# Position bias folded into the selection mask, and two levels of a recurrence copied by ScalarE, in a one-core decoder trunk

## The chip, the cores and the metric

One core of one Trainium2 chip runs the whole program. The metric is the device time of one execution in microseconds (us), the median over three runs. About 0.2% of it, some 6 us, is what a measurement of this kernel can tell from no change. The engines are TensorE (PE, with its weight loads listed apart as PEld), VectorE (DVE), ScalarE (ACT), GpSimd (POOL) and SyncE (SP), which starts most of the DMAs.

## What is computed

The reference is a decoder trunk of two layers over 1040 tokens (16 meta tokens and 1024 of the input) of width 1024. The even layer mixes with two head groups side by side, and the change is in these. All the rest (output projection, layer norms, SwiGLU, pooling mixer) is untouched.

```python
# (A) sparse attention: an indexer picks 256 keys per query, 8 heads of 64
score = einsum(relu(q_idx . k_idx), w_idx); score = where(causal, score, -inf)
_, idx = top_k(score, 256)
logits = (q . k_sel) * 64 ** -0.5
logits = logits - slope[h] * (t - idx)        # slope[h] = 2 ** -(h + 1)
p = softmax(where(idx <= t, logits, -inf))
out_a = p . v_sel
# (B) gated linear recurrence, 8 heads of 64, chunkwise
S_t = exp(logf_t) * S_(t-1) + k_t (x) v_t;  out_b = q_t . S_t
```

A softmax over keys does not change when a constant is added to a whole row of logits. So the bias of a query at position t may be written as slope * (key - c) with any c for the row.

## The kernel before, in words

The work runs in three stages, each ended by a barrier of all engines: `projection`, `mixers` and `trunk`. Queries are cut into nine tiles: tile 0 has the 16 meta tokens, tiles 1 to 8 have 128 tokens each, and tile m sees `NKEYS[m]` keys (16, 144, 272, ..., 1040).

**projection.** PE computes the indexer scores, then column slabs of the input projection (L398 to L412). Meanwhile DVE takes the 256 best keys of tiles 2 to 7 out of the scores, eight at a time (L586 to L598), and turns what is left into a mask of 0 and -1e30 (L602). For each of these six tiles POOL then blanks the part above the diagonal (`causal`, called at L331). For tiles 0 and 1 it clears the scores near the start (L285). The stage ends when the last slab is stored (ACT, L492) and POOL is through.

**mixers.** The loop runs over 72 units, 8 for each tile m: the unit (m, h) is head h of the attention of tile m and level h of the recurrence of tile m. All engines walk the same list of steps, each in its own fixed order. In a unit:

- PE: `qk` gives the logits of the head in pieces of at most 512 keys. In each piece a product over two rows (`alibi` x `rel`, in type float32r, L1003) writes the bias, and the float32 product of queries and keys (L1005) is added to it. Each float32 product shows as two records in the trace. Then `gram` (L1048; level 0 is L1038) gives one level of the recurrence's scores, then come a job on the shared bank (output, state, turned outputs), the transposes of the probabilities of the unit before (`turn`, L1063), the product with the values of the one before that (`pv`, L1085), and at h = 1, 3, 5, 7 a quarter of the output projection (L996).
- DVE: `masked` (L1265) adds mask and logits in one pass and takes the row's maximum. `scores_of` copies the level's blocks from PSUM to `S` under a mask (`copy_predicated`, L1330 and L1336). Steps of the selection for tile 8 (L1364, L1375), of the normalisation (L1398, L1401) and of the layer norm fill the rest.
- ACT: the exponential of the logits (L1123), copies of the transposes (L1132, L1135), gates.
- POOL: `carry` (L892, L895) multiplies queries and keys by the decay of the level. `gram` of the next level waits for it.

PE's `qk(i)` waits for DVE's `masked(i-1)`; `gram` of level h waits for POOL's `carry` of level h-1 (L1044) and for the copy two levels back (L1031). PE's transposes of the normalised output (L975) wait for DVE's L1401.

Ahead of the loop POOL clears buffers (L842 to L857) and makes index rows, DVE builds the level masks (L1238 to L1244) and the two bias operands (L1234, L1235, L1246, L1248), and the gates of tile 0 run through ACT and DVE (L1151 to L1168, L1314). PE's first `qk` waits for `alibi_done` (L1013).

**trunk** is the rest of the network, on the same engines.

Of the kernel before, what the change touches and what calls it, by code (L numbers as in the profile page):

```python
# [6 lines left out]
F32R = mybir.dt.float32r  # L7
I32 = mybir.dt.int32
# [52 lines left out]
def scores_at(score, m, a, b):  # L61

    return score[1][:, a:b] if m == NT - 1 else score[0][:, SC_OFF[m] + a:SC_OFF[m] + b]

# [57 lines left out]
def projection(nc, c, sem, sb, banks, ident, x, meta, w_in_v, ins, score, cqT, kaT, va, y, qz_dram, vg_dram):  # L122
# [30 lines left out]

    cq_gain = sb(c, "cq_gain_sb", [P, QC])
# [33 lines left out]
    idx_hi, idx_lo = sem("w_idx_hi"), sem("w_idx_lo")  # L188
    stored = [sem(f"stored{i}") for i in range(NS)]
# [89 lines left out]
    def _(pool):  # L279
# [5 lines left out]
        nc.gpsimd.memset(score[0][:, 0:SC_OFF[FIRST_TOPK]], 0.0).then_inc(ident_zero, 1)  # L285
        pool.wait_ge(ident_zero, 2)
# [42 lines left out]
        for i, m in enumerate(EARLY):  # L329
            pool.wait_ge(mask_done, i + 1)  # L330
            causal(m, mask_all)  # L331
# [273 lines left out]
def mixers(nc, c, sem, sb, banks, ident, x, meta, ins, score, cqT, kaT, va, y, qz_dram, vg_dram):  # L605
# [25 lines left out]
    REL0 = TILES[-1][0]  # L631
    rel_f, rel_i = probs[0:2, 0, :], probs[0:2, 1, :].bitcast(I32)
    rel = sb(c, "rel", [2, L], F32R)
    qpos_i = sb(c, "qpos_i", [2, P], I32)
    qpos = sb(c, "qpos", [2, P])
    alibi = sb(c, "alibi", [2, A_HEADS, P], F32R)
# [31 lines left out]
    w_loaded, iotas, rel_done, alibi_done = sem("wqa_loaded"), sem("iotas"), sem("rel_done"), sem("alibi_done")  # L668
# [73 lines left out]
    def tails(i):  # L742

        return sum(m == NT - 1 for m, _ in units[:i + 1])

# [95 lines left out]
    def _(pool):  # L841
# [4 lines left out]

        nc.gpsimd.iota(rel_i, pattern=[[1, L]], base=-REL0, channel_multiplier=0).then_inc(iotas, 1)
        nc.gpsimd.iota(qpos_i[:, :], pattern=[[-1, P]], base=0, channel_multiplier=0).then_inc(iotas, 1)
        nc.gpsimd.memset(vt[:, 0, :], 0.0).then_inc(pads, 1)
        nc.gpsimd.memset(gt[:, :], 0.0).then_inc(pads, 1)  # L850
        pool.wait_ge(iotas, 4)
        nc.gpsimd.affine_select(out=rel_f, in_=rel_f, compare_op=ALU.is_ge, fill=1.0, base=0,
                                pattern=[[0, L]], channel_multiplier=-1).then_inc(rel_done, 1)
        nc.gpsimd.affine_select(out=qpos[:, :], in_=qpos[:, :], compare_op=ALU.is_gt, fill=1.0, base=0,
                                pattern=[[0, P]], channel_multiplier=1).then_inc(rel_done, 1)
# [55 lines left out]
        for i, (m, h) in enumerate(steps):  # L911
# [9 lines left out]
            if norm_tile(m, h, 5) is not None:  # L921
                n0.bias(pool, norm_tile(m, h, 5))
            if i == LATE1 + 1:
                pool.wait_ge(late_mask, 1)
# [1157 lines left out]
```

## Time and profile before

| | us |
|---|---|
| median of three runs (2826.09 to 2831.94) | 2829.19 |
| the profiled execution's own time | 2828.17 |
| its span in the trace | 2826.5 |
| PE busy / VectorE busy | 2670.7 / 1298.3 |
| ScalarE busy / GpSimd busy | 843.9 / 1055.6 |
| mean granted clock of TensorE, of full speed | 0.956 |

The profiled execution is 1.0 us under the median, and 1.7 us of it lie outside the span. Engines are busy side by side, so these numbers don't add up. The trace counts time in us from the start of the span. Projection runs to about 535, mixers to about 1138, trunk to the end. "Released by" in a row (the arrow) names the instruction that ended a wait.

### The profile page before, as it was taken

The numbers are of one execution on the slowest core, as the hardware profiler recorded it, in microseconds if no ns is written. First come the engines' busy times: TensorE is split into PE (matmuls) and PEld (weight loads), VectorE is DVE, ScalarE is ACT, GpSimd is POOL, SyncE is SP. The second block draws the span as 40 slices with busy tenths as digits, with TensorE's granted clock in tenths as the row PEclk, the third lists the DMA queues.
The fourth block names the chain that finished last, engine by engine and source line by source line (L and its number), as shares of the span: only waits on it lengthen the run. The fifth ranks groups of instructions, "written<-read, shape, count | busy, mean of one in ns | idle before, by whom it ended". The sixth has DMA issues, their size and how long they took to land.

```text
span 2826.5 us, 36645 instructions
## 1 busy us (share of the span) xinstructions
PE 2670.7 (94%) x14423; PEld 2237.4 (79%) x14423; DVE 1298.3 (46%) x2480; ACT 843.9 (30%) x1377; POOL 1055.6 (37%) x628
## 2 busy tenths in 40 slices
PE   6779999689999998799999999999999999999996
PEld 5758999677777776688889877788877788888885
DVE  4889999756656542233333332232322232233224
ACT  2573222123332321332222232332332232233222
POOL 1221111354543331434333352444343344345433
PEclk8898999769999999899999998999999999999998
DMA  2001121213323213332233321333322333333331
GB/s 95 30 1 45 53 91 59 80 50 109 101 83 94 72 63 123 120 90 73 78 105 90 90 79 56 90 89 112 97 75 60 92 89 114 94 90 97 104 112 52
DMA packets 276469, 232.95 MB, mean 82 GB/s; under 512 B 10448, under 2 KB 257296, under 8 KB 276304
## 3 DMA queue, kind: packets, MB, share of 16 engines
q1 hardware_dynamic: 268112, 222.13, 26.3%
q10 hardware_dynamic: 8192, 8.52, 0.9%
q8 instruction: 115, 1.88, 0.3%
q14 instruction: 50, 0.41, 0.0%
HBM read 217.91 MB, written 12.71 MB: 82 GB/s over the span
## 4 chain that ended last, share of the span: by engine, by line
PE 56%; DMA 1%; POOL 1%; ACT 1%; DVE 1%; issue 0%; POOLq 0%; SPq 0%; ACTq 0%; DVEq 0%
PE banks L1783 33%; PE banks L1799 19%; PE banks L1816 1%; PE banks L1821 1%; PE banks L1833 1%; DMA draw<-in_w_down 1%; DMA raw<-in_w_up 1%; POOL wL L1702 0%; POOL dL L1709 0%; PE banks L1507 0%; ACT wH L1877 0%; ACT dH L1883 0%; DVE y L1485 0%; PE banks L1818 0%; DVE y L1983 0%
## 5 line engine op out<-in xcount | busy, mean ns | idle before, releaser
L1783 PE MATMUL banks<-hL,wH 128*128 128x512 f32 (+1 forms) x1760 | 620.0, 352 | 16.3 <-ACT hid L1892 14.5
L1702 POOL TENSOR_TENSOR wL<-raw,wH 128x2048 fp32r<-128x2048 f32 x88 | 406.5, 4619 | 593.8 <-ACT wH L1877 593.8
L1783 PE MATMUL banks<-hH,wL 128*128 128x512 f32 (+1 forms) x1760 | 619.0, 352 | 0.0
L1783 PE MATMUL banks<-hH,wH 128*128 128x512 f32 (+1 forms) x1760 | 616.8, 350 | 0.0
L1963 DVE TENSOR_TENSOR hid<-hid,banks 128x512 f32<-128x512 f32 (+1 forms) x110 | 64.4, 585 | 759.4 <-PE banks L1783 648.0
L1783 PEld LDWEIGHTS banks<-hL,wH 128*128 128x128 f32 x1760 | 332.3, 189 | 65.9 <-ACT hid L1892 16.0
L1783 PEld LDWEIGHTS banks<-hH,wL 128*128 128x128 f32 x1760 | 332.2, 189 | 46.3
L1783 PEld LDWEIGHTS banks<-hH,wH 128*128 128x128 f32 x1760 | 332.7, 189 | 45.0
L1709 POOL TENSOR_TENSOR dL<-draw,dH 128x1024 fp32r<-128x1024 f32 x88 | 220.8, 2509 | 373.1 <-ACT dH L1883 373.0
L1983 DVE TENSOR_TENSOR y<-y,banks 128x512 f32<-128x512 f32 (+1 forms) x340 | 233.2, 687 | 220.9 <-PE banks L1799 219.9
L1799 PE MATMUL banks<-dH,hidL 128*128 128x512 f32 (+1 forms) x748 | 304.6, 407 | 2.3 <-issue 2.3
L1799 PE MATMUL banks<-dL,hidH 128*128 128x512 f32 (+1 forms) x748 | 302.3, 404 | 0.0
L1799 PE MATMUL banks<-dH,hidH 128*128 128x512 f32 (+1 forms) x748 | 301.2, 403 | 0.0
L1883 ACT ACTIVATE dH<-draw 128x1024 fp32r<-128x1024 f32 x88 | 93.4, 1061 | 565.4 <-PE banks L1799 372.2
L892 POOL TENSOR_TENSOR qp<-qp,tot 64x256 f32<-64x256 f32 x126 | 88.7, 704 | 290.0 <-PE banks L1048 284.9
L1877 ACT ACTIVATE wH<-raw 128x2048 fp32r<-128x2048 f32 x88 | 167.9, 1908 | 41.9 <-DMA raw<-in_w_up 41.7
L1894 ACT ACTIVATE hidH<-hid 128x512 fp32r<-128x512 f32 (+1 forms) x110 | 60.5, 550 | 384.8 <-DVE hid L1963 384.8
L1799 PEld LDWEIGHTS banks<-dH,hidL 128*128 128x128 f32 (+1 forms) x748 | 141.3, 189 | 42.7 <-issue 4.3
L1799 PEld LDWEIGHTS banks<-dH,hidH 128*128 128x128 f32 (+1 forms) x748 | 141.2, 189 | 39.1
L1799 PEld LDWEIGHTS banks<-dL,hidH 128*128 128x128 f32 (+1 forms) x748 | 141.5, 189 | 36.8
L598 DVE MATCH_REPLACE8 y<-top,y 128x272 f32<-128x272 f32 (+2 forms) x192 | 143.4, 760 | 0.0
L410 PE MATMUL banks<-shared,hH 128*128 128x256 f32 (+1 forms) x648 | 137.1, 280 | 0.0
(231 smaller groups left out, 4373.0 us busy)
## 6 DMA issues: line engine op xcount, KB each, us to landing
raw<-in_w_gate SPq DMA_DIRECT2D x88, 512.0 KB, 4.8
raw<-in_w_up SPq DMA_DIRECT2D x88, 512.0 KB, 6.1
draw<-in_w_down SPq DMA_DIRECT2D x88, 512.0 KB, 3.5
w_out_part<-in_w_out SPq DMA_DIRECT2D x64, 512.0 KB, 3.9
slab<-in_w_in SPq DMA_DIRECT2D x10, 1024.0 KB, 5.8
va<-in_x SPq DMA_DIRECT2D x8, 512.0 KB, 5.1
vg_scratch<-y ACTq DMA_DIRECT2D x32, 128.0 KB, 1.7
y<-in_x SPq DMA_DIRECT2D x8, 512.0 KB, 7.2
```

The source lines that it names most:

```text
L410: last = nc.tensor.matmul(banks[0:n, i % 8, 0:SW], h[:, k, a:a + n], w[:, k, :], start=first, stop=stop)
L598: nc.vector.match_replace(at, top8[:, m, :], at, TAKEN).then_inc(topk_step, 1)
L892: nc.gpsimd.tensor_tensor(late, late, blocks[r, :, 0, :].to_broadcast([HD, n, 2 ** l]), ALU.mult) .then_inc(carried, 1)
L1702: nc.gpsimd.tensor_tensor(wL[:, ff % 2, :, :, :].rearrange("p g k f -> p (g k f)"), raw[:, :, :, :].rearrange("p g k f -> p (g k f)"), wH[ ...
L1709: nc.gpsimd.tensor_tensor(dL[:, ff % 2, :], draw[:, :], dH[:, ff % 2, :].bitcast(F32), ALU.subtract)\
L1783: last = nc.tensor.matmul(banks[:, GU + (2 * q + g) % 3, 0:n], wt[:, ff % 2, g, k, :], h[:, k, a:a + n], start=(k == 0 and part == 0), sto ...
L1799: last = nc.tensor.matmul(banks[0:n, DN + num % 3, :], h[:, (2 * g + u) % 3, t0 - ph.t0:t0 - ph.t0 + n], wt[:, u, (j % 2) * 512:(j % 2 + 1 ...
L1877: nc.scalar.activation(wH[:, ff % 2, :, :, :], raw[:, :, :, :], ACT.Copy).then_inc(w_hi, 1)
L1883: nc.scalar.activation(dH[:, ff % 2, :], draw[:, :], ACT.Copy).then_inc(d_hi, 1)
L1894: nc.scalar.activation(hidH[:, ff % 3, a - ph.t0:a - ph.t0 + n], hid[:, q % 2, 0:n], ACT.Copy)\
L1963: nc.vector.tensor_tensor(hid[:, q % 2, 0:n], hid[:, q % 2, 0:n], banks[:, GU + (2 * q + 1) % 3, 0:n], ALU.mult)\
L1983: nc.vector.tensor_tensor(at, at, banks[0:n, DN + num % 3, :], ALU.add).then_inc(y_added, 1)
```

## The change

The bias moves out of the product and into the mask. `dist` is a row 1-L, ..., -1, 0 on all partitions, and its last `NKEYS[m]` entries (`dist_of`) are key minus last query of the tile. It is added once per tile to the selection mask instead of once per head to the logits. The slope is taken out of the logits: the query weights are divided by it ahead of time, and the exponential multiplies by it (`scale`), as does the negated maximum. In tiles 0 and 1 the mask is `dist` itself.

- PE: L1003 is gone from every piece of every unit.
- projection: POOL makes `dist` (one iota, one cast of 128x1040), copies it for tiles 0 and 1, and adds it to the masks of tiles 2 to 7 at the stage's end (L344 of the new file).
- mixers, start: POOL and DVE no longer make the bias operands. ACT scales the query weights in eight instructions, and PE's first product waits for these.
- mixers, loop: POOL makes `dist` again after unit 8 and adds it to the mask of tile 8 at unit 62.
- Levels 6 and 7 of `scores_of` go from DVE to ACT (`blocks_of`): the blocks are whole squares there, so plain copies do (two of 32 partitions, then one of 64).

```diff
@@ projection, POOL
-        nc.gpsimd.memset(score[0][:, 0:SC_OFF[FIRST_TOPK]], 0.0).then_inc(ident_zero, 1)
-        pool.wait_ge(ident_zero, 2)
+        nc.gpsimd.iota(dist[:, :].bitcast(I32), pattern=[[1, L]], base=1 - L, channel_multiplier=0).then_inc(dist_done, 1)
+        pool.wait_ge(dist_done, 1)
+        nc.gpsimd.tensor_copy(dist[:, :], dist[:, :].bitcast(I32)).then_inc(dist_done, 1)
+        pool.wait_ge(dist_done, 2)
+        for m in range(FIRST_TOPK):
+            nc.gpsimd.tensor_copy(scores_at(score, m, 0, NKEYS[m]), dist_of(dist, m)).then_inc(dist_done, 1)
+        pool.wait_ge(dist_done, 2 + FIRST_TOPK)
...
         for i, m in enumerate(EARLY):
             pool.wait_ge(mask_done, i + 1)
+            at = scores_at(score, m, 0, NKEYS[m])
+            nc.gpsimd.tensor_tensor(at, at, dist_of(dist, m), ALU.add).then_inc(placed, 1)
+            pool.wait_ge(placed, i + 1)
             causal(m, mask_all)
@@ mixers, POOL
-        pool.wait_ge(iotas, 4)
...
+            if i == A_HEADS:
+                nc.gpsimd.iota(dist[:, :].bitcast(I32), pattern=[[1, L]], base=1 - L, channel_multiplier=0).then_inc(dist_done, 1)
+                pool.wait_ge(dist_done, 1)
+                nc.gpsimd.tensor_copy(dist[:, :], dist[:, :].bitcast(I32)).then_inc(dist_done, 1)
             if i == LATE1 + 1:
+                pool.wait_ge(dist_done, 2)
                 pool.wait_ge(late_mask, 1)
+                nc.gpsimd.tensor_tensor(late, late, dist_of(dist, NT - 1), ALU.add).then_inc(late_placed, 1)
+                pool.wait_ge(late_placed, 1)
@@ mixers, PE
-        pe.wait_ge(w_loaded, 16)
+        pe.wait_ge(w_scaled, A_HEADS)
...
         def scores_of(m, h, a, kn, at):
             t0, n = TILES[m]
-            nc.tensor.matmul(logits[0:n, at:at + kn], alibi[:, h, 0:n], rel[:, REL0 - t0 + a:REL0 - t0 + a + kn],
-                             start=True, stop=False)
             return nc.tensor.matmul(logits[0:n, at:at + kn], qaT[:, m % 2, h, 0:n], kaT[:, h // 2, a:a + kn],
-                                    start=False, stop=True)
+                                    start=True, stop=True)
@@ mixers, ACT
+        act.wait_ge(w_loaded, 16)
+        for h in range(A_HEADS):
+            at = w_qa[:, :, h * HD:(h + 1) * HD]
+            nc.scalar.activation(at, at, ACT.Copy, scale=HD ** -0.5 / SLOPES[h]).then_inc(w_scaled, 1)
...
-            nc.scalar.activation(at, at, ACT.Exp, bias=nmax[0:n, i % 2, 2:3], accum_out=sums[0:n, m % 2, h:h + 1])\
+            nc.scalar.activation(at, at, ACT.Exp, bias=nmax[0:n, i % 2, 2:3], scale=SLOPES[h], accum_out=sums[0:n, m % 2, h:h + 1])\
...
+        def blocks_of(i):
+
+            m, h = units[i]
+            l = h - 1
+            act.wait_ge(gram_psum, i + 1)
+            act.wait_ge(gram_read, i)
+            for b in range(P // 2 ** h):
+                r = slice(b * 2 ** h, b * 2 ** h + 2 ** l)
+                src = banks[r, GRAM + h % 2, :].rearrange("p (h n t) -> p h n t", h=8, t=2 ** l)[:, :, b, :]
+                last = nc.scalar.activation(S[r, m % 2, :, b * 2 ** h + 2 ** l:(b + 1) * 2 ** h], src, ACT.Copy)
+            last.then_inc(gram_read, 1)
...
+            if i < NU and h in PLAIN:
+                blocks_of(i)
@@ mixers, DVE
-        dve.wait_ge(iotas, 2)
-        nc.vector.tensor_copy(rel_f, rel_i).then_inc(iotas, 1)
-        nc.vector.tensor_copy(qpos[:, :], qpos_i[:, :]).then_inc(iotas, 1)
...
-        dve.wait_ge(rel_done, 2)
-        linked(nc.vector.tensor_copy(rel[:, :], rel_f))
-        for h in range(A_HEADS):
-            last = nc.vector.tensor_scalar(alibi[:, h, :], qpos[:, :], 2.0 ** (-8.0 * (h + 1) / A_HEADS), None, ALU.mult)
-        last.then_inc(alibi_done, 1)
...
-            if i < NU:
+            if i < NU and h not in PLAIN:
```

How the order of the instructions changes is shown at three places. In the rows the name of a line is that of its own file.

On PE, a unit of tile 7 in the mixers loop (`w_out_part` is the output projection's quarter, `kaT` and `qaT` are keys and queries, `qp` and `key` the recurrence's operands, `ident` marks transposes), before:

```order
L996 MATMUL banks<-w_out_part,oT 128x256 x8
L1003 MATMUL banks<-rel,alibi 128x512
L1005 MATMUL banks<-kaT,qaT 128x512
L1003 MATMUL banks<-rel,alibi 128x400
L1005 MATMUL banks<-kaT,qaT 128x400
L1048 MATMUL banks<-qp,key 128x128 x4
L979 MATMUL banks<-ident,o_tok 128x128 x4
```

and with the change:

```order
L1010 MATMUL banks<-w_out_part,oT 128x256 x8
L1017 MATMUL banks<-kaT,qaT 128x512
L1017 MATMUL banks<-kaT,qaT 128x400
L1058 MATMUL banks<-qp,key 128x128 x4
L993 MATMUL banks<-ident,o_tok 128x128 x4
```

The two bias products are gone, and float32 products follow one another from the quarter of the output projection to the recurrence's.

On DVE, the start of the mixers stage, from the last level mask to the first gate (`pT` holds index tables there), before:

```order
L1241 TENSOR_SCALAR pT<-pT 128x128
L1242 SCALAR_TENSOR_TENSOR masks<-pT 128x128
L1244 TENSOR_SCALAR masks<-pT 128x128
L1246 CAST rel<-probs 2x1040
L1248 TENSOR_SCALAR alibi<-qpos 2x128 x8
L1314 SCALAR_TENSOR_TENSOR key_arg<-zt,lnw 128x512
L1317 SCALAR_TENSOR_TENSOR lnw<-zt,lnw 128x512
```

and with the change:

```order
L1265 TENSOR_SCALAR pT<-pT 128x128
L1266 SCALAR_TENSOR_TENSOR masks<-pT 128x128
L1268 TENSOR_SCALAR masks<-pT 128x128
L1332 SCALAR_TENSOR_TENSOR key_arg<-zt,lnw 128x512
L1335 SCALAR_TENSOR_TENSOR lnw<-zt,lnw 128x512
```

Nine instructions ahead of the first gate are gone, and two casts (L1234, L1235) at the head of this queue.

On POOL, the end of the projection stage (`y` holds the scores there), before:

```order
L308 TENSOR_TENSOR slab1L<-slab,shared 128x2048
L291 AFFINE_SELECT y<-y 128x128 x6
L86 UNCONDITIONAL_BRANCH
L88 ISA
L840 UNCONDITIONAL_BRANCH
L842 MEMSET zt 128x512
```

and with the change:

```order
L320 TENSOR_TENSOR slab1L<-slab,shared 128x2048
L344 TENSOR_TENSOR y<-y 128x272
L303 AFFINE_SELECT y<-y 128x128
L344 TENSOR_TENSOR y<-y 128x400
L303 AFFINE_SELECT y<-y 128x128
L344 TENSOR_TENSOR y<-y 128x528
L303 AFFINE_SELECT y<-y 128x128
```

Six adds, of 272 to 912 elements a partition (3552 together), now stand between the masks and the stage's end.

## Rows read from the trace of the kernel before

**Rows 1.** busy time by stage: stretch, PE PEld DVE ACT POOL busy, PEclk, DMA, GB/s

```profile
586.90:648.40 61.50, 58.79 (x300) 47.28 (x300) 34.84 (x70) 16.12 (x55) 32.58 (x49) 0.67 0.13 39
648.40:1087.40 439.00, 434.13 (x2606) 334.13 (x2607) 237.76 (x465) 136.19 (x339) 177.55 (x233) 1.00 0.27 84
```

**Rows 2.** waits on PE, 550:1090; columns: who for whom, total, times, longest

```profile
PE banks L1003 <- DVE alibi L1248: 11.2, 1, 11.2
PE banks L1048 <- POOL key L895: 9.9, 5, 3.0
```

**Rows 3.** line L1003 on PE: its forms, and its busy time in the stage

```profile
L1003 PE MATMUL banks<-rel,alibi x120: 168/445/501, 553.5 to 1083.7; 2*128 2x512 f32 x48, 2*128 2x144 f32 x16, 2*128 2x272 f32 x16, 2*128 2x400 f32 x16
...
550.00:1150.00 600.00, 48.96 (x120) 21.66 (x120) 0.93 0.28 88
```

**Rows 4.** timeline of PE, one unit of tile 7 (start, us, what)

```profile
951.71 0.49 PE L1003 MATMUL banks<-rel,alibi 2*128 2x512 f32 x1
952.13 1.13 PE L1005 MATMUL banks<-kaT,qaT 128*128 128x512 f32 x2
953.19 0.44 PE L1003 MATMUL banks<-rel,alibi 2*128 2x400 f32 x1
953.56 0.94 PE L1005 MATMUL banks<-kaT,qaT 128*128 128x400 f32 x2
954.34 1.07 PE L1048 MATMUL banks<-qp,key 128*128 128x128 f32 x8
```

**Rows 5.** timeline of PE, 1087:1091

```profile
1087.40 3.62 PE L996 MATMUL banks<-w_out_part,oT 128*128 128x256 f32 x16
1090.86 1.04 PE L1063 MATMUL banks<-ident,probs 128*16 128x128 f32 x8
```

**Rows 6.** timelines of DVE, POOL and ACT, start of the mixers stage

```profile
539.99 7.38 DVE L1241 TENSOR_SCALAR pT<-pT 128x128 int32<-128x128 int32 x1
...
551.51 0.69 DVE L1246 CAST rel<-probs 2x1040 fp32r<-2x1040 f32 x1
...
553.32 0.67 DVE L1314 SCALAR_TENSOR_TENSOR key_arg<-zt,lnw 128x512 f32<-128x512 f32 x1
...
536.87 0.98 POOL L847 IOTA probs<- 2x1040 int32 x1
...
539.75 1.11 POOL L852 TENSOR_SCALAR_AFFINE_SELECT probs<-probs 2x1040 f32<-2x1040 f32 x1 [0.23 <-DVE qpos L1235]
...
545.49 1.79 POOL L857 MEMSET qp<- 128x2048 f32 x1
...
544.75 0.63 ACT L1158 ACTIVATE lnw<-u 128x512 f32<-128x512 f32 x1
```

**Rows 7.** timelines of ACT and POOL around the stage's end, then a POOL group

```profile
532.65 0.33 ACTq L492 DMA_DIRECT2D vg_scratch<-y  x1
...
523.91 2.74 POOL L291 TENSOR_SCALAR_AFFINE_SELECT y<-y 128x128 f32<-128x128 f32 x6 [35.03 <-DVE y L602]
535.55 0.53 POOL L842 MEMSET zt<- 128x512 f32 x1 [8.91 <-POOLq L89]
...
L1491 POOL TENSOR_TENSOR y<-y,n_b 128x1024 f32<-128x1024 f32 x6 | 14.1, 2354 | 18.9 <-DVE y L1485 18.9
```

**Rows 8.** masked copies of L1336 on DVE (ns min/median/max)

```profile
L1336 DVE COPY_PREDICATED S<-masks,banks x63: 675/726/1327, 560.5 to 1084.8; 128x512 f32<-128x512 uint8 x63
```

**Rows 9.** timelines of POOL and PE, tile 2

```profile
655.56 0.74 POOL L895 TENSOR_TENSOR key<-key,tot 128x256 f32<-128x256 f32 x1
...
656.45 1.13 PE L1048 MATMUL banks<-qp,key 128*128 128x128 f32 x8
```

**Rows 10.** timelines of DVE and PE, tile 4

```profile
777.95 0.69 DVE L1401 TENSOR_TENSOR on<-on,gt 128x512 f32<-128x512 f32 x1
...
778.79 0.63 PE L975 MATMUL banks<-ident,on 128*128 128x128 f32 x4
```

**Rows 11.** timeline of PE, tile 1

```profile
591.61 2.08 PE L1048 MATMUL banks<-qp,key 128*128 128x128 f32 x8
```

More of the change, by code:

```diff
@@ L63, in scores_at, with dist_of @@
     return score[1][:, a:b] if m == NT - 1 else score[0][:, SC_OFF[m] + a:SC_OFF[m] + b]
+def dist_of(dist, m):
+    return dist[:, L - NKEYS[m]:L]
 def key_chunks(n):
@@ L152, in slab_raw @@
         return slab_first[:, j, :, :] if j < 2 else slab[:, j % 2, :, :]
+    dist = y[:, 3:5, :].rearrange("p m f -> p (m f)")[:, 0:L]
     cq_gain = sb(c, "cq_gain_sb", [P, QC])
@@ L188, in projection @@
     idx_hi, idx_lo = sem("w_idx_hi"), sem("w_idx_lo")
+    dist_done, placed = sem("dist_done"), sem("placed")
     stored = [sem(f"stored{i}") for i in range(NS)]
@@ L630, in mixers @@
     o_tok = sb(c, "o_tok", [P, 2, A_WIDTH])
[L631 to L636, printed above, removed]
+    dist = sb(c, "dist", [P, L])
+    SLOPES = [2.0 ** (-8.0 * (h + 1) / A_HEADS) for h in range(A_HEADS)]
     zt = sb(c, "zt", [P, W])
@@ L666, in mixers @@
     rsh = sb(c, "rsh", [P, 8])
-    w_loaded, iotas, rel_done, alibi_done = sem("wqa_loaded"), sem("iotas"), sem("rel_done"), sem("alibi_done")
+    w_loaded, w_scaled, late_placed = sem("wqa_loaded"), sem("wqa_scaled"), sem("late_placed")
+    dist_done = sem("late_dist_done")
     qk_done, qk_tail, nmax_raw, nmax_tail, nmax_done = (sem("qk_done"), sem("qk_tail"), sem("nmax_raw"),
@@ L744, in tails @@
         return sum(m == NT - 1 for m, _ in units[:i + 1])
+    PLAIN = (LEVELS - 1, LEVELS)
     def halves(ap, l):
@@ L845, in _ @@
         nc.gpsimd.iota(it_t, pattern=[[1, P]], base=0, channel_multiplier=0).then_inc(iota_done, 1)
-        nc.gpsimd.iota(rel_i, pattern=[[1, L]], base=-REL0, channel_multiplier=0).then_inc(iotas, 1)
-        nc.gpsimd.iota(qpos_i[:, :], pattern=[[-1, P]], base=0, channel_multiplier=0).then_inc(iotas, 1)
         nc.gpsimd.memset(vt[:, 0, :], 0.0).then_inc(pads, 1)
         nc.gpsimd.memset(gt[:, :], 0.0).then_inc(pads, 1)
-        pool.wait_ge(iotas, 4)
[L852 to L855, printed above, removed]
         for dst in (qaT, S, state, added, qp):
@@ L1011, in qk @@
                 pe.wait_ge(shared_done, nth["qa", m])
-            if i == 0:
-                pe.wait_ge(alibi_done, 1)
             if i:
@@ L1179, in off_shared @@
                     to = qaT[r, m % 2, :, 0:n].rearrange("p (f two) t -> p two f t", two=2)[:, par]
-                    ins_ = nc.scalar.activation(to, four(src)[r, :, 0:n], ACT.Copy, scale=HD ** -0.5)
+                    ins_ = nc.scalar.activation(to, four(src)[r, :, 0:n], ACT.Copy)
             if what == "kT":
@@ L1277, in masked @@
                 peak = 1
-            nc.vector.tensor_scalar(nmax[0:n, i % 2, 2:3], nmax[0:n, i % 2, peak:peak + 1], -1.0, None, ALU.mult)\
+            nc.vector.tensor_scalar(nmax[0:n, i % 2, 2:3], nmax[0:n, i % 2, peak:peak + 1], -SLOPES[h], None, ALU.mult)\
               .then_inc(nmax_done, 1)
```

## The prediction

> **What bounds the kernel now.** I first cut the trace by stage. The change touches only what lies before 1138 us, so the trunk, 1688 us of the span, is taken as it is. Within the mixers the table of busy time [rows 1] shows PE busy 58.8 of 61.5 us in tile 1 and 434.1 of 439.0 us in tiles 2 to 8, while DVE has work for 54% and POOL for 40% of the latter. Busy PE proves little, since records overlap. So I looked at the waits: from 550 to 1090 us PE waited 11.2 us for the bias operands, once, ahead of the first unit, and 9.9 us for POOL's decays, five times [rows 2], all in tile 0. The timeline of a unit says the same: each PE instruction starts where the one before lets it, with no gap but those that the weight loads make [rows 4]. So from tile 1 on the order on PE is the clock of the stage, and an instruction taken off PE is worth its whole distance to the next one. In tile 0 the loop runs PE, POOL, PE, and PE has time to spare.
>
> **The bias products.** There are 120 of them, 48.96 us busy [rows 3]. A record overlaps the next one: the piece of 512 is recorded with 0.49 us, but the next instruction starts 0.42 us after it [rows 4], 0.07 less. 48.96 - 120 x 0.07 = 40.6 us, less the eight of tile 0 that PE's waits hide (about 1 us): **40 us** if nothing but these distances goes. That is the lower bound.
>
> More may go. The 512 keys of L1005 take 952.13 to 953.19, 1.06 us, and the whole unit's logits 951.71 to 954.34, 2.63 us for 912 keys [rows 4]. Where float32 products follow each other without a float32r one in between, eight of 256 columns (16 records) take 1087.40 to 1090.86, 3.46 us, or 0.43 us for 256 columns [rows 5]; by that rate 912 columns take 1.54 us. The unit then saves 1.09 us, where the two distances of L1003 give 0.42 + 0.37 = 0.79. The rest is weight loads which the change of type seems to leave in the open, before and after each bias product. Scaled by 1.09/0.79 the 40 us become **55 us**. The entry into the first bias product of a unit may hide another 0.1 us in each of 64 units: 61 us, the upper bound. I take 55, since the rate of rows 5 is one of the same type on the same engine at the same clock.
>
> The Trainium skill, "TensorE: Matmul & The Clock Gate", table at the head: the queue of TensorE can pull a weight load ahead of matmuls in flight. Rows 5 agree with that, rows 4 don't at the two changes of type; if the rule held there too, the gain would be nearer 40 than 55.
>
> **What comes late next.** Two other engines get close to PE. POOL's decays: in tile 2 L895 ends at 656.30 and PE's product on it starts at 656.45 [rows 9], so in such units (some seven in tiles 1 to 3, those without a long job on PE) the saving of about 0.5 us is lost in part: -2 us. DVE's normalisation: in tile 4 L1401 ends at 778.64 and PE's transposes start at 778.79 [rows 10], the same 0.15 us that stands for a release. There the saving of the two units before is lost in part: 1 to 1.5 us in each of tiles 1, 4 and 5, -3.5 us. In tile 8 PE waits for DVE's maximum in each unit, and DVE will be late in a few: -1.5 us. Together 7 us given back, so 48 of the 55 arrive.
>
> **The start of the mixers.** DVE's first shift (L1241) lasted 539.99 to 547.37, where the fourteen instructions behind it take 4.1 us together, and it ended with POOL's run of memsets, at 547.28 [rows 6]: it got through only when POOL paused. POOL now does without an iota of 0.98 us and a select of 1.11 us [rows 6], two short ones of the same kinds and the wait for DVE between them, about 1 us more. Its memsets end at about 544.2. From the end of the first shift to L1246 DVE takes 551.51 - 547.37 = 4.1 us, which stays; from L1246 to L1314 it takes 1.8 us, which goes [rows 6]. So the first gate starts at 548.4 in place of 553.32: **-4.9 us**. All the chain of tile 0 hangs on this gate. What could fill the place: ACT's eight scalings of the query weights. They are 128 elements each in a row of 512-element instructions at 0.63 us [rows 6], so between 2 us (a third of that each, near what 128 elements should need) and 5 us for all. ACT's last gate ended at 545.38 and now ends up to 2 to 4 us later, since PE's product for the first queries comes behind the scalings; at 2 it is hidden, at 4 it costs 1 us. I take it as hidden.
>
> The Trainium skill, "SBUF — State Buffer", section "Who interferes with whom": GpSimd and a two-port DVE instruction lock each other out for one whole instruction. The trace shows more: the 7.38 us outlast four of five memsets. By the rule the shift would wait for one memset, 1.8 us, the masks would be through before ACT's gates, and the gain here would be about 6 us, not 4.9.
>
> **The end of the projection.** POOL's adds cost 2354 ns per 1024 elements [rows 7], so 3552 elements take 8.2 us, the six selects 2.7 as before [rows 7], and six hand-overs about 0.15 each. From 523.9 that ends at 535.7. Before, the last store was issued at 532.65 and POOL's first instruction of the next stage came at 535.55 [rows 7]; with some 2 us for the store to land, the barrier takes about 0.9. POOL is now last by about 1 us: **+1.2 us** (0 to +3). If the slabs did not cover it the price would be all 9 us.
>
> **Priced at nothing.** POOL's `dist` at the program's start lies ahead of its first long instruction, which waits for the indexer's weights; in the loop it lies behind unit 8 and at unit 62, where POOL is idle half the time; if that cover went, each would delay one decay by 2 to 3 us. The copies of levels 6 and 7: DVE loses 18 of about 0.73 us [rows 8], 13 us, but PE doesn't wait for them. ACT gets about 1.3 us in two units of each tile and is 31% busy [rows 1]. Behind its copies wait the transposed probabilities, which PE reads a whole unit later (3.5 us or more). If that cover went, it would be at most 9 x 1.3 = 12 us, and as a gain I see none: 0.
>
> **Sum.** 55 - 7 + 4.9 - 1.2 = 51.7. 2828.17 - 51.7 = 2776.5; the median stood 1.0 higher than this execution, so I forecast **2777 us** for the median.
>
> **Rivals.**
>
> - *Only the distances go, and the neighbours hold the rest.* The weight loads stay in the open and DVE and POOL take back 10 us: 40 - 10 + 4 - 2 = 32, so 2797. For it: two engines with 40 to 54% of work in fixed orders, and releases of 0.15 us already seen in two places. Against it: rows 5. Chance 0.22.
> - *The low clock holds on: slower.* The granted clock is 0.67 from 586.9 to 648.4, although PE is busy nearly throughout, and 1.00 after [rows 1]; at the low level (1.2 GHz) eight records of L1048 take 2.08 us, at the high one (2.4 GHz) 1.07 [rows 11, 4]. The bias products are work for PE; without them tiles 1 to 3 have less in the same order, and the rise at 648 could come later. Each us of PE's work done at the low level costs up to one more. The point from which it decides: some 52 us of work, that is the low level held through tile 2. Held through tile 3 (100 us of work) it gives 2777 + 80, about 2850. Against it: the shorter units pack the remaining products denser. The Trainium skill, "TensorE: Matmul & The Clock Gate", "What's actually happening", has the clock follow how busy PE has been; by that alone PE should have been at the high level in tile 1, and it wasn't. Chance 0.03.
> - *The clock rises earlier.* 0.67 over 61.5 us leaves about 20 us to be won in tile 1; half of it gives 2767. Chance 0.07.
> - *The parts cancel, or the bias products cost nothing*: in the trace nothing hides them from tile 1 on. Chance 0.01.
>
> **How the numbers follow.** Forecast 0.67, the rivals as above. The forecast's own range is 61 - 5 + 6 = 62 to 40 - 7 + 2 = 35, so 2766 to 2793; with most of the first rival and half of the clock's gain it becomes 2760 to 2800. Faster by over 0.2% (about 6 us, what a measurement can tell) 0.96, within 0.01, slower 0.03.
>
> **What would show it.** L1003 absent; a unit of tile 7 with its 912 keys in 1.5 to 1.6 us; L1048 and L975 with more waits, a few us in all; the first gate on DVE at about 549.5; the stage's first POOL instruction at about 536.7; the high clock from about 640. It is wrong if the logits' distance per unit shrinks by 0.8 us or less, if PE's waits in tiles 1 to 8 grow by over 12 us, if the low level outlasts tile 1, or if the trunk's length changes.

## The result, and the profile after

The changed kernel takes 2786.1 us (median of four runs, 2781.0 to 2788.7) beside 2827.6 us for the kernel before: ratio 0.9849, 95% interval 0.9829 to 0.9869. It is 41.5 us faster, where 52 were forecast: the forecast was 2777, 9 us under the result, and the kernel before came out 1.6 us lower with its fourth run. The range of 2760 to 2800 holds the result. The profiled execution took 2784.3 us.

The page of the changed kernel, its busy time (PE had 2670.7 before):

```profile
span 2782.6 us, 36417 instructions
...
PE 2620.8 (94%) x14303; PEld 2224.0 (80%) x14303; DVE 1284.3 (46%) x2451; ACT 854.9 (31%) x1412; POOL 1067.2 (38%) x636
```

PE lost 49.9 us of busy time and the span only 43.9. To see where, I cut both traces at the same events: the first gate (L1314 before, L1332 now), the first product of the logits of each tile, and the first PE instruction of the trunk. Tile 8 is taken up to the first product of its last unit, so seven of its eight units. The table is worked out from the start times of those rows.

| us | before | after |
|---|---|---|
| first gate starts at | 553.3 | 548.1 |
| gate to trunk | 585.2 | 546.0 |
| trunk | 1688.0 | 1688.5 |
| tile 1 | 51.6 | 44.7 |
| tile 2 | 48.0 | 49.1 |
| tile 3 | 51.3 | 51.5 |
| tiles 4 to 7 | 267.8 | 237.3 |
| tile 8, seven units | 73.7 | 69.8 |

The loop gave 39.1 us and what lies ahead of it 5.3. Tiles 4 to 7 gave 30.5 of the loop's, tiles 2 and 3 nothing, and seven units of tile 8, which has the most keys, 3.9, less than half of the 9.3 of tile 7.

Busy time by stretch, tile 1 and then tiles 2 to 8 of the changed kernel (columns as in [rows 1], whose first stretch runs on into tile 2):

```profile
583.20:627.90 44.70, 40.63 (x217) 33.76 (x216) 24.78 (x51) 14.89 (x51) 30.49 (x47) 0.70 0.10 28
627.90:1035.70 407.80, 394.72 (x2537) 328.30 (x2537) 237.58 (x461) 143.56 (x361) 180.74 (x235) 0.98 0.30 93
```

PE's granted clock was 1.00 in [rows 1] from 648.4 on. Now it is 0.98 over tiles 2 to 8: some of the time is at the low level (1.2 GHz). PE is also idle more. Its waits from 550 to 1090 us, changed kernel, answering [rows 2]:

```profile
PE banks L1058 <- POOL key L902: 11.5, 8, 3.0
PE banks L989 <- DVE on L1419: 11.2, 6, 3.4
PE banks L1017 <- DVE nmax L1283: 5.1, 8, 1.1
PE banks L1010 <- DMA w_out_part<-in_w_out: 4.4, 3, 2.0
...
PE banks L1073 <- ACT pT L1149: 1.0, 2, 0.5
```

The alibi wait is gone, POOL's decays stand at 11.5 us for 9.9, and the normalised output at 7.8 us in place of 2.7: the other 3.4 of the 11.2 stand behind the loop, and the kernel before has the same 3.4 there, outside the window of [rows 2]. The last line is new, and small. ScalarE's new order, from which it comes, will turn out to go with the largest loss.

A unit of tile 7 on PE, the counterpart of [rows 4]:

```profile
919.05 1.69 PE L1017 MATMUL banks<-kaT,qaT 128*128 128x512 f32 x4
920.58 1.07 PE L1058 MATMUL banks<-qp,key 128*128 128x128 f32 x8
```

One row holds both pieces: 919.05 to 920.58, 1.53 us for 912 keys. It was 2.63.

The start of the mixers, changed kernel: DVE, POOL and ACT, the counterpart of [rows 6] and of the POOL rows of [rows 7]:

```profile
538.90 0.32 DVE L1265 TENSOR_SCALAR pT<-pT 128x128 int32<-128x128 int32 x1
...
539.58 1.46 DVE L1265 TENSOR_SCALAR pT<-pT 128x128 int32<-128x128 int32 x1
...
541.40 1.46 DVE L1265 TENSOR_SCALAR pT<-pT 128x128 int32<-128x128 int32 x1
...
548.06 0.69 DVE L1332 SCALAR_TENSOR_TENSOR key_arg<-zt,lnw 128x512 f32<-128x512 f32 x1 [0.61 <-ACT lnw L1172]
...
533.11 2.10 POOL L344 TENSOR_TENSOR y<-y 128x912 f32<-128x912 f32 x1
535.36 0.29 POOL L303 TENSOR_SCALAR_AFFINE_SELECT y<-y 128x128 f32<-128x128 f32 x1
536.84 0.52 POOL L856 MEMSET zt<- 128x512 f32 x1 [1.19 <-POOLq L94]
...
539.08 1.88 POOL L864 MEMSET qaT<- 128x2048 f32 x1
540.90 1.87 POOL L864 MEMSET S<- 128x2048 f32 x1
...
540.14 1.70 ACT L1128 ACTIVATE w_qa<-w_qa 128x128 f32<-128x128 f32 x8 [2.01 <-DMA w_qa<-in_w_uq]
```

POOL ends the projection stage now and its first memset comes at 536.84 (535.55 in [rows 7]). DVE's shifts are no longer shut out for 7.38 us: each takes 1.46 us at most beside a memset of 1.88, and then gets through. The gate now waits 0.61 us for ACT, so ACT is what sets it.

The masked copies that stay on DVE, and the block copies on ACT, against [rows 8]:

```profile
L1354 DVE COPY_PREDICATED S<-masks,banks x45: 681/722/1336, 555.2 to 1021.1; 128x512 f32<-128x512 uint8 x45
```

```profile
L1223 ACT ACTIVATE S<-banks x27: 356/374/590, 578.6 to 1041.2; 32x256 f32<-32x256 f32 x18, 64x512 f32<-64x512 f32 x9
```

In tile 2 PE, DVE and POOL of the changed kernel stand like this, where [rows 9, 10] had shown releases of 0.15 us:

```profile
657.00 1.05 PE L1058 MATMUL banks<-qp,key 128*128 128x128 f32 x8
659.77 0.63 PE L989 MATMUL banks<-ident,on 128*128 128x128 f32 x4 [1.71 <-DVE on L1419]
...
660.66 1.47 PE L1095 MATMUL banks<-va,pT 16*128 16x64 f32 x6
662.06 4.79 PE L1010 MATMUL banks<-w_out_part,oT 128*16 128x256 f32 x16
...
656.43 1.52 DVE L1416 TENSOR_TENSOR on<-on,rsh 128x512 f32<-128x512 f32 x1
657.99 1.63 DVE L1419 TENSOR_TENSOR on<-on,gt 128x512 f32<-128x512 f32 x1
...
656.37 1.04 POOL L913 TENSOR_TENSOR state<-state,tot 128x512 f32<-128x512 f32 x1
657.49 1.59 POOL L915 TENSOR_TENSOR state<-state,state_added 128x512 f32<-128x512 f32 x1
```

DVE's two products took 1.5 and 1.6 us beside POOL's (0.69 in [rows 10], without them), PE waited 1.71 us, and right behind that wait its products ran slow: the quarter of the output projection took 4.79 us, where [rows 5] have 3.62. So this wait cost more than its length. Not every such wait does: in e6 below the same wait of 1.71 us stands in tile 2, and the tile ran at a granted clock of 1.00. The Trainium skill, "SBUF — State Buffer", section "Who interferes with whom", says that a DVE instruction with two inputs in SBUF contends with a GpSimd instruction that reads SBUF; these rows agree.

### The profile page after: what moved, and what is told of

It is laid out like the page before. It is cut to its first block, busy times and chain, and to the rows that moved or that the text cites. A ratio compares the mean times of both kernels' runs of the same rounds, so it can differ in the third digit from the quotient of the medians.

```text
span 2782.6 us, 36417 instructions
## 1 busy us (share of the span) xinstructions
PE 2620.8 (94%) x14303; PEld 2224.0 (80%) x14303; DVE 1284.3 (46%) x2451; ACT 854.9 (31%) x1412; POOL 1067.2 (38%) x636
## 4 chain that ended last, share of the span: by engine, by line
PE 56%; DMA 1%; POOL 1%; ACT 1%; DVE 1%; issue 0%; POOLq 0%; SPq 0%; ACTq 0%; DVEq 0%
PE banks L1801 34%; PE banks L1817 19%; PE banks L1834 1%; PE banks L1839 1%; PE banks L1851 1%; DMA draw<-in_w_down 1%; DMA raw<-in_w_up 1%; POOL dL L1727 1%; POOL wL L1720 0%; PE banks L1525 0%; ACT wH L1895 0%; ACT dH L1901 0%; DVE y L1503 0%; PE banks L1836 0%; DVE y L2001 0%
```

## The experiments

Twelve kernels ran, in three groups, each group on a chip of its own. All ratios are to the kernel before, timed on the same chip at the same time; its median was 2830.4 us for e0, e1, e5 and e6, 2827.2 for e2, e3, e8 and e9, and 2829.7 for e4, e10, e11 and e12. So medians of different groups can't be set against each other to within 3 us. Gate and loop (gate to trunk) are from each profile.

| run | median us | ratio, 95% interval | gate | loop | tiles 2, 3, 8 |
|---|---|---|---|---|---|
| e0_after_again | 2782.9 | 0.9832 [0.9814, 0.9850] | 549.0 | 545.9 | 49.1, 51.6, 69.8 |
| e1_bias_only | 2777.7 | 0.9808 [0.9790, 0.9826] | 549.0 | 538.6 | 48.5, 49.3, 64.7 |
| e5_on_first | 2776.1 | 0.9814 [0.9793, 0.9836] | 548.7 | 535.6 | 47.2, 49.3, 65.0 |
| e6_adds_dve | 2778.0 | 0.9811 [0.9791, 0.9831] | 545.4 | 545.3 | 48.1, 51.5, 69.8 |
| e2_blocks_only | 2828.7 | 1.0003 [0.9994, 1.0012] | 552.8 | 589.2 | 48.0, 51.3, 78.8 |
| e3_bias_f32 | 2925.9 | 1.0343 [1.0325, 1.0361] | 552.7 | 684.6 | 49.6, 55.2, 95.0 |
| e4_bias_twice | 2849.0 | 1.0068 [1.0053, 1.0084] | 552.0 | 610.3 | 48.4, 52.7, 81.9 |
| e10_rows128 | 2800.5 | 0.9897 [0.9882, 0.9913] | 553.1 | 556.6 | 47.5, 50.2, 67.9 |
| e9_turned_first | 2776.9 | 0.9818 [0.9804, 0.9831] | 547.7 | 538.2 | 48.5, 49.3, 64.7 |
| e8_all_three | 2774.6 | 0.9814 [0.9801, 0.9828] | 546.2 | 544.0 | 46.5, 48.6, 64.7 |
| e11_turned_adds | 2770.0 | 0.9798 [0.9783, 0.9813] | 544.5 | 537.9 | 47.3, 49.3, 64.7 |
| e12_turned_adds_on | 2775.3 | 0.9818 [0.9803, 0.9833] | 545.2 | 537.9 | 46.7, 48.6, 64.7 |

**e0_after_again** is the changed kernel itself.

> The changed kernel once more, as the mark for the others on the same chip. Expected 2781 to 2789 us. If the low clock in tiles 2, 3 and 8 belongs to the program, the 64-column products of tile 8 take the double time again; if it is chance, they don't, and the time is up to 5 us lower.

2782.9 us, and the tiles agree with the first profile to 0.1 us. The slow stretches in tiles 2, 3 and 8 belong to the program.

**e1_bias_only**: the changed kernel with levels 6 and 7 back on DVE.

```diff
-            if i < NU and h in PLAIN:
-                blocks_of(i)
...
-            if i < NU and h not in PLAIN:
+            if i < NU:
```

> The bias part alone: levels 6 and 7 stay masked copies on VectorE. Theory (the gain is the bias products alone, VectorE has room there): within 3 us of the changed kernel, and TensorE's waits for ScalarE's transposed probabilities (1.0 us) go. Rival 1 (ScalarE's copies hold up the transposed probabilities): faster by 4 us or more. Rival 2 (VectorE's relief pays): slower by 5 us or more, with more waits for VectorE in tiles 1 to 5.

5.2 us faster than the repeated change. The intervals of the two ratios overlap, but not the runs (2774.0 to 2779.1 and 2781.1 to 2785.3). In the profile the loop is 7.3 us shorter, in tiles 2, 3 and 8. The copies on ScalarE, which I had priced at nothing, cost in the place where they stand.

**e5_on_first**: the normalisation (L1416, L1419) right behind the maximum on DVE, the rest as changed.

> The changed kernel with VectorE's two normalisation steps of a tile right behind the maximum of the logits instead of at the unit's end. Theory (what was given back in tiles 1 to 5 is TensorE's wait for these steps, 7.8 us, and the low clock that follows the longest of them, 2 to 3 us): 7 to 10 us faster than the changed kernel, no wait for L1419 but the one after the loop, units 5 of tiles 2 and 3 in 8 us instead of 10.3. Rival (the next thing in the queue takes its place: gates, copies of blocks or of transposes late): 0 to 3 us, with new waits of the same sum.

6.8 us faster by the median, though its runs (2771.1 to 2785.2) spread over those of e0; the profile is of the fastest. PE's waits for the normalised output fell from 11.2 to 3.4 us (what is left stands behind the loop), tile 1 from 44.7 to 41.3, and the slow stretches of tiles 3 and 8 are gone too, with ScalarE's copies still in place. PE still waits twice for `pT` here:

```profile
PE banks L1073 <- ACT pT L1149: 1.0, 2, 0.5
```

A new wait of 3.9 us for ACT's `oT` and 2.5 us more in tiles 4 and 5 take a part back.

**e6_adds_dve**: the six adds of `dist` to the masks on DVE, behind its last mask.

> The changed kernel with the six adds of positions to the masks on VectorE behind the masks instead of on GpSimd. Theory (GpSimd was last at the stage's end by 1.3 us): the mixers stage starts at 535.5 as before the change instead of 536.8, the whole is 1 to 2 us faster, which only the trace can tell. Rival (something else ends that stage): it starts at 536.8 again.

4.9 us faster than the repeated change; the first gate comes 3.5 us earlier, the loop is the same. So POOL's adds at the stage's end cost some 3 us: 3.5 in this pair of profiles, 2.7 by the means given below.

**e2_blocks_only**: the kernel before with ScalarE's copies alone.

> The kernel before, with levels 6 and 7 of the recurrence's scores copied as whole blocks by ScalarE; the bias products stay. My theory, from the last runs: in the changed kernel these copies cost about 5 us, and chiefly because PE then slips to the low clock in tiles 3 and 8, which needs the lighter load that the missing bias products leave. Then here, where PE is loaded more, they cost little: between -2 and +3 us against the kernel before (2828 to 2833), tile 8 at 73 to 75 us. Rival 1: the copies cost by their place in ScalarE's order (the transposed probabilities come later in two units of each tile), whatever the clock does: +5 us or more here too, spread over the tiles. Rival 2: they gain here, since DVE's maximum ends earlier and PE waits for it in tile 8: -3 us or more.

2828.7 beside 2827.2: no difference. But my reason fell. In the profile, which is of the slowest of the eleven runs (2832.9), tile 8 did slip to the low clock (78.8 us for 73.7), without any lighter load on PE and without any wait of PE for `pT`. Tile 1 was shorter, 46.8 us for 51.6. That is no gain of the copies: tile 1 took 47.4 us in e4 and 51.2 in e3, where nothing was moved to ScalarE. Whether tile 8 slips in the other ten runs too is not shown.

**e9_turned_first**: the same work on ScalarE in another order.

```diff
-            if i < NU and h in PLAIN:
-                blocks_of(i)
             if 1 <= i <= NU:
                 turned(i - 1)
                 if units[i - 1][0] == NT - 1:
                     turned_rest(i - 1)
+            if i < NU and h in PLAIN:
+                blocks_of(i)
```

> The changed kernel with ScalarE's block copies moved behind the copies of the transposed probabilities, in the same two units of each tile. The work on ScalarE is the same, only its order differs. Theory 1: the copies cost what they cost because the transposed probabilities stand behind them and PE waits for them (0.5 us in a unit, and what the clock makes of it): then the waits for the transposed probabilities go, and the time falls by 3 to 5 us, to 2778 to 2780. Theory 2: it is the copies' contention or the earlier idle moments of PE that matter, not this order: 2782 to 2784, with tile 8 still at about 69.8 us. Theory 3: PE now waits for the copied blocks instead, in the product that reads level 6 or 7: 2785 or more.

2776.9 us. That is 6.0 less than the repeated change, but on another chip: by the two ratios it is 4 us, and their intervals overlap, so the times alone don't settle it. The profile does for the tiles: 2, 3 and 8 are those of e1 to the tenth. Theory 1 holds so far: not the copies cost, their place does. Nor does it gain anything that VectorE is rid of 18 copies: e9 and e1 take the same time. ACT and PE of the changed kernel, tile 2:

```profile
670.81 0.74 ACT L1223 ACTIVATE S<-banks 32x256 f32<-32x256 f32 x2
671.58 0.27 ACT L1146 ACTIVATE pT<-banks 16x128 f32<-16x128 f32 x1
671.75 0.36 ACT L1149 ACTIVATE pT<-banks 128x256 f32<-128x256 f32 x1
...
672.25 0.49 PE L1073 MATMUL banks<-ident,probs 128*16 128x128 f32 x3 [0.49 <-ACT pT L1149]
```

and of e9_turned_first at the same place:

```profile
670.41 0.25 ACT L1146 ACTIVATE pT<-banks 16x128 f32<-16x128 f32 x1
670.57 0.36 ACT L1149 ACTIVATE pT<-banks 128x256 f32<-128x256 f32 x1
670.84 0.74 ACT L1223 ACTIVATE S<-banks 32x256 f32<-32x256 f32 x2
...
671.21 0.49 PE L1073 MATMUL banks<-ident,probs 128*16 128x128 f32 x3
```

The next transposes write over the bank that `pT` is copied out of (`pe.wait_ge(t_act, i)` in `turn`), so a late copy holds PE. That happens twice, 0.49 and 0.51 us in tiles 2 and 3. Of the 8.0 us between the two kernels in these tiles (0.6 in tile 2, 2.3 in tile 3, 5.1 in tile 8) only 1.0 is this wait; nearly all the rest is PE at the low level. In tile 8, columns as before, the changed kernel:

```profile
972.00:988.00 16.00, 15.49 (x80) 13.54 (x80) 3.62 (x8) 3.89 (x7) 2.53 (x3) 0.70 0.00 1
...
977.80 0.39 PE L982 MATMUL banks<-state,qp 128*128 128x64 f32 x2
...
978.88 0.64 PE L982 MATMUL banks<-state,qp 128*128 128x64 f32 x2
```

and e9_turned_first over the same 16 us, in which it is 3.3 us further on in the program:

```profile
972.00:988.00 16.00, 14.48 (x99) 12.66 (x100) 7.01 (x17) 3.09 (x7) 4.70 (x6) 1.00 0.21 66
```

PE falls to the low level in the middle of a job of products of 64 columns, 0.39 us a pair and then 0.64. Up to there the two kernels' PE rows agree to 0.01 us in length for 25 us back, waits included. So putting the order right removed the low clock in tile 8, but no row near it shows what brings it on.

The short waits for `pT` are not enough to bring it. e5 has both of them (0.48 and 0.51 us) with the same order on ScalarE, and its tiles 3 and 8 ran at 1.00. e2 has the low clock in tile 8 and no such wait. The profiles of the change, e0, e6 and e2 have the low clock in tile 8; those of the kernel before, e1, e5 and e8 to e12 don't; e3 and e4, whose bias products are longer or doubled, have some of it with the old order (0.53 from 1074 to 1085 us in e4, in tile 8). In tile 3 the low stretch of the change lies ahead of that tile's wait for `pT`, behind one of 1.18 us for the normalised output at 710.05 (0.83 granted from 710 to 720); the same wait is in e9 (1.17 us, at 709.01), whose clock stayed at 1.00. What brings the low clock on stays open.

**e3_bias_f32, e4_bias_twice, e10_rows128** ask why a bias product cost more than its columns. All three are the kernel before with one edit:

```diff
@@ e3: float32 in place of float32r
-    rel = sb(c, "rel", [2, L], F32R)
-    alibi = sb(c, "alibi", [2, A_HEADS, P], F32R)
+    rel = sb(c, "rel", [2, L])
+    alibi = sb(c, "alibi", [2, A_HEADS, P])
@@ e4: each bias product twice
+            for again in range(2):
+                nc.tensor.matmul(logits[0:n, at:at + kn], alibi[:, h, 0:n], rel[:, REL0 - t0 + a:REL0 - t0 + a + kn],
+                                 start=True, stop=again == 0)
@@ e10: 128 rows in place of 2, the others zero
+    rel = sb(c, "rel", [P, L], F32R)
+    alibi = sb(c, "alibi", [P, A_HEADS, P], F32R)
...
+        linked(nc.vector.memset(rel[:, :].bitcast(mybir.dt.float32), 0.0))
+        linked(nc.vector.memset(alibi[:, :, :].bitcast(mybir.dt.float32), 0.0))
```

> The kernel before, with the two operands of the bias product in float32 in place of float32r: the same 120 products, but no change of type between them and the products of queries and keys. Theory: a float32r product between float32 ones lays weight loads open before and after it, about 0.2 us each; a float32 product of two rows costs twice the columns' time but no such load. Then in the unit of tile 7 the piece of 512 keys is 0.87 us long instead of 1.06, its bias product about 0.85 instead of 0.42, the unit's logits about 3.1 us instead of 2.63, and the whole about 20 to 30 us slower than before. Rival: the type has nothing to do with it, and any further product of other weights costs its load: then the 512 keys stay at 1.06 us, the unit's logits are about 3.4 us, and the whole is 40 us or more slower.

Part of a unit of tile 6 in e3_bias_f32:

```profile
952.50 1.12 PE L1003 MATMUL banks<-rel,alibi 2*128 2x512 f32 x2
953.55 1.13 PE L1005 MATMUL banks<-kaT,qaT 128*128 128x512 f32 x2
954.61 0.72 PE L1003 MATMUL banks<-rel,alibi 2*128 2x272 f32 x2
```

Without any change of type the 512 keys still take 1.06 us (953.55 to 954.61). My cause, the change of type, is refuted. The bias product in float32 takes 1.05 us (952.50 to 953.55) where 0.85 was expected, so it too costs 0.2 us beyond its columns. The whole is 98.7 us slower, in the open range of the rival (40 or more) and far above the theory's 20 to 30. A good part of it is this:

```profile
740.00:1085.00 345.00, 345.00 (x1707) 250.20 (x1707) 153.36 (x286) 83.82 (x201) 110.51 (x150) 0.88 0.22 70
```

PE is busy in all of these 345 us, waits for nobody, and is granted 0.88. In the kernel before the same tiles ran at 1.00. Twelve hundredths of 345 us are 41 us, my estimate of what the clock took; the rest is the longer products.

> The kernel before, with each bias product issued twice (the second starts the sum anew, so the values are the same): 120 more products over two rows, and none of them stands at a change between two rows and 128. What it tells apart is why a bias product cost more than its columns: 512 columns at four passes are 0.85 us, and the product of queries and keys took 1.06 although in the changed kernel it takes 0.85. Theory A (a product whose weights have another number of rows than those before it can't have its load pulled ahead; the float32 run has ruled out the type): two products over two rows follow each other at the columns' rate, so the second is 0.21 to 0.25 us for 512 columns, the first stays at 0.42, and the whole is 120 x 0.2 = 15 to 25 us slower than before. Theory B (every such product has its load in the open): the second takes 0.42 us as well, and the whole is 40 us or more slower.

The first piece of a unit of tile 6 in e4_bias_twice, two bias products (in one row) and the product of queries and keys:

```profile
929.85 0.73 PE L1004 MATMUL banks<-rel,alibi 2*128 2x512 f32 x2
930.50 1.13 PE L1006 MATMUL banks<-kaT,qaT 128*128 128x512 f32 x2
```

0.65 us for two where one took 0.42 [rows 4], so the second, which has the same two rows as the one ahead of it, adds 0.23; theory B wanted 0.84 for the two. The second has the same weights too, but it is not spared its load: the trace has 240 weight loads for the 240 products. The whole is 19.3 us slower, within the 15 to 25 of theory A.

> The kernel before, with the two operands of the bias product widened from 2 to 128 rows, the other 126 all zero: the same 120 products in float32r, with the same columns and the same sum, now over as many rows as the products of queries and keys. It adds two fills on DVE (about 2 us) at the start of the mixers, ahead of the first gate. Theory A (the change in the number of rows lays the loads open): in the unit of tile 7 the bias product of 512 keys takes 0.21 to 0.25 us in place of 0.42, the product of queries and keys 0.87 in place of 1.06, the unit's logits 1.9 to 2.0 us in place of 2.63, and the whole is 20 to 35 us faster than before, so half or more of what the change won in the loop comes without removing a single product. Theory B (the load of any further product is in the open): the unit's logits stay at 2.6 us or grow, and the whole is 0 to 5 us slower.

A unit of tile 7 in e10_rows128:

```profile
931.98 0.58 PE L1003 MATMUL banks<-rel,alibi 128*128 128x512 f32 x1
932.40 1.02 PE L1005 MATMUL banks<-kaT,qaT 128*128 128x512 f32 x2
...
934.10 1.08 PE L1048 MATMUL banks<-qp,key 128*128 128x128 f32 x8
```

2.12 us (931.98 to 934.10) in place of 2.63, a little more than the 1.9 to 2.0 expected, and the whole 29.2 us faster than before, with all 120 products still there. The single pieces don't start as expected (0.42 us from the bias product to the next, where 0.21 to 0.25 was expected); the unit and the whole do come out. The weight loads of the same rows show what changed. The kernel before [rows 4], then e10_rows128:

```profile
951.71 0.18 PEld L1003 LDWEIGHTS banks<-rel,alibi 2*128 2x128 f32 x1 [0.33 <-issue]
952.13 0.30 PEld L1005 LDWEIGHTS banks<-kaT,qaT 128*128 128x128 f32 x2 [0.24 <-issue]
```

```profile
931.95 0.19 PEld L1003 LDWEIGHTS banks<-rel,alibi 128*128 128x128 f32 x1
932.16 0.42 PEld L1005 LDWEIGHTS banks<-kaT,qaT 128*128 128x128 f32 x2
```

Before, each of these loads starts only when its product's own record starts (951.71 and 952.13, as in [rows 4]). With 128 rows the load for the keys starts at 932.16, 0.24 us ahead of its product at 932.40 and while the bias product runs. Theory A holds: a product over two rows among products over 128 has its weight load, and that of the next one, in the open. Only 2 and 128 rows were tried. The Trainium skill, "TensorE: Matmul & The Clock Gate", section "The mechanism", says in one place that a load overlaps a product in flight only when the two are in different groups of rows, and in another that the weight buffer in the background serves as well. The rows here are against the first: loads hide between products over the same 128 rows (the load at 932.16) and are laid open where the number of rows changes; the measurement decides.

**e8_all_three, e11_turned_adds, e12_turned_adds_on** put the single gains together: e8 is e1, e5 and e6 in one, e11 is e9 and e6, e12 is e11 and e5.

> The changed kernel with three edits that each gained alone: levels 6 and 7 back on DVE as masked copies, the normalisation on DVE right behind the maximum, the six adds of the distances on DVE. If the gains add up (5.1, 6.7 and 4.7 us over the repeated change): 2782.9 - 16.5 = 2766. Theory: the first two both work by keeping PE at the high clock in tile 8, so that gain counts once: 2782.9 - 5.1 - 6.7 - 4.7 + 5 = about 2771. Rival: with DVE's 18 masked copies back, the normalisation in front of them puts the copies late and PE waits for them: 2774 to 2778.

> The changed kernel with two edits: ScalarE's block copies behind the transposed probabilities (alone 2776.9) and the six adds of the distances on DVE (alone 4.7 us under the repeated change; the first gate 3.5 us earlier). They act in different places, the order in the loop and the stage's start, so they should add up: 2776.9 - 3.5 to 4.7 = 2772 to 2773.5, with tile 8 at 64.7 us and the first gate at about 545.5. Rival: the earlier start ends in tile 1 at the low clock, which then lasts longer: 2775 to 2777.

> The run before this one with the normalisation on DVE right behind the maximum too. That edit alone made tile 1 3.4 us and tile 2 2.0 us shorter and tiles 4 and 5 2.5 us longer in all; what it won in tiles 3 and 8 is already had. If this holds: 2772.5 - 2.9 = about 2769.5. Rival: DVE no longer copies levels 6 and 7 here, so the losses of tiles 4 and 5 go as well: 2767. Other rival: with the earlier start the gain in tile 1 is not repeated, as in the run with all three edits, where tiles 4 and 5 took 59.5 and 60.3 us: 2773 or more.

e8: 2774.6, within its rival's range, but hardly for its reason. Tiles 4 and 5 are 59.5 and 60.3 us long (55.5 and 57.4 in the change). 1.0 and 1.5 us of that stand in e5 and e12 as well (56.5 and 58.9), with the wait for `oT`; the rest goes with the low clock, 0.94 and 0.97 granted in e8 and 1.00 in e12. e11: 2770.0, a little better than expected, with the gate at 544.5. e12: 2775.3, not the 2769.5 expected. Its loop is as long as e11's (537.9): tiles 1 to 3 won 2.2 us and tiles 4 and 5 lost 2.5. The 5 us between the medians are thus not in the loop. The trunks of the two profiles differ by 4 us, and I have no reason for that; the same trunk took 1684.8 to 1691.9 us in the fourteen profiles, and 1684.8 and 1688.5 in the two of the changed kernel itself. **e11_turned_adds** is the fastest version that ran: 57 us under the kernel before by its ratio, and 10 to 14 under the change, by the ratio of e0 or of the first result.

## Why the prediction was right in kind and 9 us short

- **What bounds the kernel.** Right. The order on PE is the clock of the loop, and L1003 gave its distance and more.
- **The bias products, 55 us.** The size was right, the cause wrong. The unit of tile 7 takes 1.53 us, forecast 1.54 by the rate of [rows 5]. With ScalarE's order put right (e9) the loop is 47.0 us shorter than before, against 55 - 7 = 48. So close an agreement is part luck: tile 1 alone took 46.8 to 51.6 us in the profiles with all bias products over two rows, and the kernel before has the 51.6. But "weight loads which the change of type seems to leave in the open" does not hold: e3 kept one type and left them open, e10 kept the types apart and had them mostly gone. It is the change between 2 and 128 rows. e10's 29.2 us show that over half of the 55 was this, and less than half the products' own columns.
- **What comes late next, 7 us.** Right in size, partly wrong in place. In tiles 1 to 3 POOL's decays cost 1.4 us (forecast 2). The normalisation cost 5.1 us more in tiles 1 to 5 (forecast 3.5), but 2.9 of it in tiles 2 and 3, where I had expected none, because DVE's L1416 and L1419 met POOL's there; tile 1's wait stayed at 2.8. The maximum in tile 8 cost 1.1 us (1.5). That is 7.6. Not named in the prediction were short waits for `S`, `o_tok`, `k_tok` and `state_added` in tiles 1 to 5, 2.2 us, while one of 0.9 for `oT` went.
- **Start of the mixers, -4.9 us.** Too small. From the stage's first memset to the first gate it took 17.8 us in each of four kernels with the old start (the kernel before, e2, e3, e4) and 11.2 to 11.3 in five with the new (the change, e0, e1, e5, e9): -6.5. The mechanism was wrong: I let the first shift again wait for all memsets, but the shifts passed between them. That is the rule of one whole instruction which the prediction cites from the Trainium skill, "SBUF — State Buffer", section "Who interferes with whom", and its estimate of 6 was the better one. In the kernel before the shift had outlasted all five memsets, not four of them. ACT's eight scalings took 1.70 us, under my 2; ACT's `lnw` is what now holds the gate.
- **End of the projection, +1.2 us.** Too small as well. One pair of profiles gives +1.3, but the stage's first memset came at 532.9 to 535.6 in five kernels with the old end (mean 534.5) and at 536.5 to 537.8 in five with POOL's adds (mean 537.3): +2.7. The six adds took 9.4 us, for 8.2. e6's gate came 3.5 us earlier by moving them. The two errors cancel: 3.7 us net were forecast, and the means give 3.8.
- **Priced at nothing: ScalarE's copies.** This step failed, and with it the forecast's last 8 us. I wrote that the transposed probabilities behind the copies are read a whole unit later. PE reads them then, but its next transposes need the bank emptied at once. The direct price is 1.0 us; e9 shows 8.0 us in tiles 2, 3 and 8, by the low clock, and some 4 us in the time by the ratios. Why the low clock came with this order is open. I had named the low level as a rival only for tiles 1 to 3 and as one long stretch; it came as three short ones. The bound of 12 us was right, the value of 0 was not.
- **Rivals.** "Only the distances go" would have given 0.79 us per unit; 1.10 went. The low clock did not last past tile 1 as a whole. The rise came somewhat earlier: tile 1 is 6.9 us shorter, though only 2.1 against the tile 1 of e2. The trunk did not change beyond what its profiles differ by.

In sum, 48 us of the loop forecast, 39.1 measured; of the missing 9, 8 are ScalarE's order.

## What to carry to other kernels

Before a copy is put ahead of another on an engine with time to spare, look for both things that wait for the other: who reads its result, and who needs its source emptied. Look at the clock behind a wait on PE as well as at the wait: the order that brought half a microsecond of waiting twice went along with 8 us in the loop, though the waits by themselves (e5) did not bring them. And a thin product (two rows) between full ones is dear for its neighbours: widening it with zeros to 128 rows gave back over half of what removing it did, at the price of two fills.

## What was not expected of the hardware

- A product over 2 rows between products over 128 costs about 0.2 us more than its columns, and so does the one behind it (at 512 columns 0.42 us, where a second one adds 0.23, and 1.06 for 0.85); between products over the same rows nothing of this is seen.
- PE, busy for 345 of 345 us, was granted 0.88 when the products over two rows ran in float32 (e3). Being busy does not keep the high level; the rows show the low one in products behind a wait of 1.7 us, in a job of products of 64 columns, and behind the two-row products of e3.
- DVE and POOL hand over to each other between instructions in one kernel (1.46 us per shift), and in the other the first shift stood 7.38 us while POOL went through five memsets [rows 6]. Which of the two happens was not tried.
- Profiles of kernels with the same projection stage differ by up to 2.6 us at its end, so a term of 1 us at a barrier can't be read from one pair.
